# Dilated attention: where the query products wait for the gate, how a head's scores are issued, and where the query copy stands

## The reference

```
def _dilated_mixer(h, k_sh, v_sh, in_w, out_w):
    q, z = jnp.split(h @ in_w, [DIL_Q_WIDTH], axis=-1)      # 3 groups x 8 heads x 128, and 1024
    ...
    for g, (window, dilation) in enumerate(((128, 1), (512, 4), (2048, 16))):
        o, lse = _dilated_window_attention(q[:, :, g], k_sh[:, :, g], v_sh[:, :, g],
                                           window, dilation, slopes[g])
    ...
    wts = jax.nn.softmax(jnp.stack(lses, 2), axis=2)
    o = jnp.einsum("blghe,blgh->blhe", o, wts).reshape(bsz, L, DIL_OUT_WIDTH)
    o = o.astype(h.dtype) * jax.nn.silu(z)
    return o @ out_w
```

## Time and profile before

| | |
|---|---|
| median of 3 runs | 3319.02 us (3318.02 to 3320.58) |
| profiled execution, first to last instruction | 3321.7 us (no other time of it is given) |
| granted TensorE clock, mean | 0.982 |
| TensorE matmuls busy | 3210.1 us (97%) |
| VectorE busy | 2397.5 us (72%) |
| ScalarE busy | 1577.0 us (47%) |
| GpSimd busy | 663.6 us (20%) |
| DMA | 667.85 MB, mean 201 GB/s |

### The profile page before, as it was taken

The page is one execution under the profiler, slowest core; times in us unless marked ns, Lnnn a source line. Parts: engine busy times, 40 slices in busy tenths (PEclk is TensorE's granted clock), DMA queues, the critical chain, the costliest instruction groups (busy, mean ns, idle before and its releaser), DMA issues.

```text
span 3321.7 us, 64507 instructions
## 1 busy us (share of the span) xinstructions
PE 3210.1 (97%) x21980; PEld 2947.2 (89%) x21980; DVE 2397.5 (72%) x3846; ACT 1577.0 (47%) x2226; POOL 663.6 (20%) x635
## 2 busy tenths in 40 slices
PE   8989999999999999999999999999998999999997
PEld 7888999999889998899878879999997879988895
DVE  6665459399878997799999776335898877554455
ACT  4655444433444344433444555545775444344442
POOL 1040039300111001100000116886221111100000
PEclk9999999999999999999999999999999999999998
DMA  6434554666787668866656874666776877755443
GB/s 205 151 98 146 170 164 154 192 207 214 239 267 226 215 218 259 265 200 214 198 178 189 266 249 133 181 189 209 240 236 194 275 235 258 243 188 173 138 128 140
DMA packets 185794, 667.85 MB, mean 201 GB/s; under 512 B 24176, under 2 KB 24400, under 8 KB 184384
## 3 DMA queue, kind: packets, MB, share of 16 engines
q1 hardware_dynamic: 149840, 545.91, 51.9%
q0 software_dynamic: 35824, 120.19, 11.6%
HBM read 663.83 MB, written 2.18 MB: 201 GB/s over the span
## 4 chain that ended last, share of the span: by engine, by line
PE 87%; DVE 5%; issue 3%; ACT 2%; POOL 2%; DMA 0%; DVEq 0%; POOLq 0%; ACTq 0%; SPq 0%
PE PS L562 15%; PE PS L564 15%; PE PS L563 15%; PE PS L906 7%; PE PS L908 7%; PE PS L910 7%; POOL w_lo L476 2%; PE PS L635 2%; PE PS L633 2%; PE PS L634 2%; PE PS L1086 2%; PE PS L1088 2%; PE PS L1090 2%; PE PS L861 1%; PE PS L786 1%
## 5 line engine op out<-in xcount | busy, mean ns | idle before, releaser
L1254 ACT ACTIVATE w_hi<-raw 128x1024 fp32r<-128x1024 f32 x1032 | 1092.9, 1060 | 1574.1 <-PE PS L564 915.0
L1769 DVE TENSOR_TENSOR w_lo<-raw,w_hi 128x1024 fp32r<-128x1024 f32 x872 | 1065.3, 1223 | 577.0 <-ACT w_hi L1254 569.9
L562 PE MATMUL PS<-xt_hi,w_hi 128*128 128x256 f32 x4608 | 1329.8, 289 | 21.7 <-POOL w_lo L476 7.3
L563 PE MATMUL PS<-xt_lo,w_hi 128*128 128x256 f32 x4608 | 1310.0, 284 | 0.0
L564 PE MATMUL PS<-xt_hi,w_lo 128*128 128x256 f32 x4608 | 1309.8, 284 | 0.0
L562 PEld LDWEIGHTS PS<-xt_hi,w_hi 128*128 128x128 f32 x4608 | 890.5, 193 | 32.1 <-issue 22.2
L563 PEld LDWEIGHTS PS<-xt_lo,w_hi 128*128 128x128 f32 x4608 | 890.7, 193 | 0.5
L564 PEld LDWEIGHTS PS<-xt_hi,w_lo 128*128 128x128 f32 x4608 | 890.1, 193 | 0.0
L476 POOL TENSOR_TENSOR w_lo<-raw,w_hi 128x1024 fp32r<-128x1024 f32 x160 | 406.4, 2555 | 372.7 <-ACT w_hi L1254 372.6
L906 PE MATMUL PS<-w_hi,st_hi 128*128 128x512 f32 x1024 | 401.9, 392 | 0.3
L910 PE MATMUL PS<-w_lo,st_hi 128*128 128x512 f32 x1024 | 398.8, 389 | 0.0
(11 more groups left out here) (396 smaller groups left out, 3489.0 us busy)
## 6 DMA issues: line engine op xcount, KB each, us to landing
raw<-in_u_emb SPq DMA_DIRECT2D x256, 512.0 KB, 3.7
raw<-in_v_emb SPq DMA_DIRECT2D x256, 512.0 KB, 4.4
ada<-in_ada_w POOLq DMA_DIRECT2D x240, 256.0 KB, 4.4
raw<-in_xbc SPq DMA_DIRECT2D x96, 512.0 KB, 3.6
raw<-in_z SPq DMA_DIRECT2D x80, 512.0 KB, 3.7
raw<-in_q SPq DMA_DIRECT2D x64, 512.0 KB, 3.5
raw<-in_a_out SPq DMA_DIRECT2D x64, 512.0 KB, 4.2
raw<-in_k SPq DMA_DIRECT2D x48, 512.0 KB, 4.3
```

Of the source, the lines that this page charges most:

```text
L562: pe.matmul(o, w_h, x_h, start=start, stop=False, skip_group_check=True)
L563: pe.matmul(o, w_h, x_l, start=False, stop=False, skip_group_check=True)
L1254: act.activation(w_hi[:, u, :], raw[:, u, :], ACT.Copy).then_inc(hi_done, 1)
L1769: dve.tensor_tensor(w_lo[:, u, :], raw[:, u, :], w_hi[:, u, :].bitcast(F32), ALU.subtract)\
```

## The change

The edits are four. TensorE's waits for the last group of values and for the gate's SiLU move from ahead of the query products to the scores of head 0; ahead of the products stays a wait for the first five groups of values. `head_scores` takes a list of groups and is called twice for each head, with groups 0 and 1 ahead of `head_turn` and group 2 behind it, each call waiting for its own query copies; `head_scored` now counts two for a head, and its two readers are adapted. On ScalarE the query copy moves ahead of the second rounding of its iteration. On VectorE the last head's `head_low` moves one step earlier, behind the fifth `low` of the loop.

```diff
@@ -1152,16 +1152,18 @@
             token_columns(0, FIRST_BODY["z2"], 4, 1, source=shifted_source)
-            pe.wait_ge(sem("v2_out"), 2 * DG)
-            pe.wait_ge(sem("z2_out"), 1)
-
-            def head_scores(h):
-
-                pe.wait_ge(act_free, 2 + ACT_BLOCKS["q2"] + 3 * h + 3)
-                if h:
+            pe.wait_ge(sem("v2_out"), 2 * DG - 1)
+
+            def head_scores(h, groups):
+
+                if h == 0:
+                    pe.wait_ge(sem("v2_out"), 2 * DG)
+                    pe.wait_ge(sem("z2_out"), 1)
+                else:
                     pe.wait_ge(sem("dist_added"), h)
                     pe.wait_ge(sem("pT2_done"), h)
-                for g in range(DG):
+                pe.wait_ge(act_free, 2 + ACT_BLOCKS["q2"] + 3 * h + groups[-1] + 1)
+                for g in groups:
@@ -1210,9 +1212,10 @@
                 if k == 2:
+                    head_scores(h, (0, 1))
                     if h:
                         head_turn(h - 1)
-                    head_scores(h)
+                    head_scores(h, (2,))
@@ -1707,7 +1710,7 @@
                 if i % 3 == 0 and i:
-                    act.wait_ge(sem("head_scored"), i // 3)
+                    act.wait_ge(sem("head_scored"), 2 * (i // 3))
@@ -1742,8 +1745,8 @@
                 if h and k == 0:
                     head_exp(h - 1)
+                head_query(i)
                 high(f + 1 + i // 2, 2 * (i % 2) + 1)
-                head_query(i)
@@ -2640,7 +2643,7 @@
-                dve.wait_ge(sem("head_scored"), h + 1)
+                dve.wait_ge(sem("head_scored"), 2 * h + 2)
@@ -2718,7 +2721,7 @@
                 if i == 3:
                     head_outputs(DH - 1)
-                if i == 5:
+                if i == 4:
                     head_low(DH - 1)
```

## The result

The changed kernel takes 3300.1 us (median of four runs, 3297.3 to 3300.7), where the kernel before takes 3319.8 (median of four runs, 3318.0 to 3323.7) on the same chip. The ratio is 0.9939, with a 95% interval of 0.9927 to 0.9951, so the time fell by 0.5 to 0.7%. The forecast was 3299.3 us in a range of 3294.5 to 3306.5.

What follows compares the result with a forecast made beforehand. TensorE was taken to bound the kernel, carrying 87% of the chain. Gains of 6.9 + 8.2 + 4.6 = 19.7 us off 3319.0 gave 3299.3 us, range 3294.5 to 3306.5.

Steps and rivals of the forecast that it cites:

- The boundary: Gate's last product to first query product: 6.9 us gained, 4.7 of idle and 2.2 of clock.
- The fifth tile's split: Weight tile rounded behind the SiLU: split to about 3059.4, needed at 3063.9, so 4.5 us of slack.
- The heads: Scores in two goes, copy moved up: 8.2 us gained, 1.7 in head 0, 5.7 in heads 1 to 6, 0.8 in head 7.
- where does this stall go: Heads 1 to 6: scores gain 1.48 us, but VectorE's maxima and ScalarE's exponential leave 0.95 us net each.
- The new wait: Before the probabilities' transposes: 0.53 us, from T + 7.99 to T + 8.52, T being the end of a head's third product.
- The copy's move: Query copy ahead of second rounding: delays rounding, split and raw load by 0.27 us in 24 products, hidden by 10.9 us of slack.
- The output tile: Output tile 6, last head's head_low earlier: 4.6 us gained, 2.98 of idle and 1.62 of clock.
- Heads gaining in full without a new wait: Rival: maxima start once scores are there, heads gain 12.05 us in place of 8.2; 3295.5 us, chance 0.15.
- The boundary's other releaser: Rival: the idle at the first query product is not the SiLU's, gain there 0; 3306.2 us, chance 0.06.
- the falling clock among the heads: Rival: clock falls at seven new short waits, 1.6 us each, 11.3 us given back; 3310.6 us, chance 0.03.
- The starved ring: Rival: query products wait for weight tiles, each 0.27 us longer; 3325.5 us, chance 0.02.
- The smaller gain: Head 0, table load with a drain, a switch at about 2.66 us: gain 0.4 instead of 1.7 us.

Runs made afterwards that it cites:

- only_wait: The kernel before with only TensorE's moved waits for the values and the gate's SiLU; ratio 0.9971 against the kernel before.
- gate_copied: The kernel before with a plain copy for the gate's SiLU; gap at the first query product 3.23 us instead of 4.66, no ratio.
- maxima_first: The changed kernel with VectorE taking a head's maxima ahead of the second split of its third product; ratio 0.9927 against the kernel before.
- one_go: The changed kernel with a head's scores in one go behind the transposes, query copy still moved up; ratio 0.9944 against the kernel before.
- copy_behind: The changed kernel with the query copy back behind the second rounding, scores still in two goes; ratio 0.9938 against the kernel before.
- only_low: The kernel before with only the last head's head_low one step earlier; ratio 0.9985 against the kernel before.
- maxima_table: The changed kernel with the maxima ahead of that split and a small exponential at the third query product; 3294.1 us, ratio 0.9915 against the kernel before.
- only_heads: The kernel before with only the scores in two goes and the moved query copy; ratio 0.9970 against the kernel before.
- low_back: The changed kernel with the last head's head_low put back one step later; stretch to output tile 7 22.60 us, no ratio.

## Why the prediction was right

**The boundary, 6.9 us forecast, 6.90 measured.** Both halves hold: the start is one spacing behind the gate's product, and the clock stays at 1.00. only_wait shows that the moved wait does it alone, gate_copied that the SiLU was the releaser. The fifth tile's split runs from 3055.77 to 3057.0 in the changed kernel and its product is due at 3050.11 + 11.5 = 3061.6, so the cover holds with 4.6 us.

**The heads, 8.2 us forecast, 8.88 measured.** The step "where does this stall go" was the right one: of the 1.48 us that the scores gain, a part is lost again to the exponential. Its size was off by little. I put the transposes of the probabilities at T + 8.52 and they come at T + 8.43, a net gain of 1.04 us instead of 0.95 in six heads. In head 0 it is 1.75 for 1.7 (9.14 for 9.17), in head 7 0.92 for 0.8. The new wait, counted as in the prediction from where TensorE is ready (T + 7.94, the start in maxima_first; I had T + 7.99) to T + 8.43, is 0.49 us for 0.53; the 0.34 of the list is not the same measure.

**The copy's move** I treated together with the two goes, as 0 for the weights and as 0.27 us in VectorE's chain. The first holds: TensorE waits for no weights from the boundary on. The second holds as well (the maxima come 0.21 us later, T + 3.04 against T + 2.83), and the runs show what I had not drawn from it. Against the kernel before, the copy moved alone (one_go) takes 7.49 us off the heads, the two goes alone (copy_behind) take off 9.77, and the two together 8.88. The edits do the same work twice, and the second one takes back 0.89.

**The output tile, 4.6 us forecast, 4.57 measured** and 4.56 in only_low. Of it 3.0 is idle; the rest is the clock behind it. The clock fell there in both traces of the kernel before, but that share is not as firm as I wrote (below).

**The sum** is 6.90 + 8.88 + 4.57 = 20.4 us in one pair of traces, and 19.7 us between the medians; the forecast was 19.7. The terms met their stretches; that the medians meet the sum to a tenth is chance, as the runs of one kernel lie 3 to 6 us apart.

**The rivals.** Heads gaining in full without a new wait did not come, but maxima_first makes it come: 12.4 us (178.95 to 166.54) against the 12.05 that I had worked out for that rival. The boundary's other releaser is refuted by gate_copied, the falling clock among the heads by a window of 170 us at 1.00 with eight waits in it. That window also does not bear out, for waits of this length, what the Trainium skill, "TensorE: Matmul & The Clock Gate", section "A second HAM failure mode: psum-queue depth-cycling", says of short idles. The starved ring did not show even in maxima_first, where the second split comes over 4 us later. The smaller gain that I had worked out from the Trainium skill, "ScalarE: Activation LUTs", section "What ACT_TABLE_LOAD costs", was 0.4 us in head 0; it gained 1.75, and the load in maxima_table costs 1.30 us from its start to the next activation, with no drain to be seen.

## What to carry to other kernels

When a stall is removed, follow the chain of every engine to the next point where the bound engine meets it, with the instructions in the order in which each engine has them; here that gave the new wait to within 0.1 us, and its root was a weight split standing ahead of the maxima on VectorE. Two edits that cover the same wait don't add, and the one that delays another engine's queue can cost: try each alone. Take the length of a wait between matmuls from the spacing of their starts, since a list that counts from a modelled end gives less (0.34 for 0.5 us here). Look at what is queued behind a long activation that nobody needs soon, and place the wait for it where its result is first read or its banks first overwritten.

## What was not expected of the hardware

The same idle of 2.9 us before output tile 6 lies in seven traces, and three different clocks followed it. In only_wait (twice) it was 1.00 throughout. In the kernel before (twice) and in gate_copied it fell within the first 0.9 us behind the restart. In only_heads and low_back the first matmul was already at the lower level: the spacing to the next is 0.56 us, where it is 0.30 at full clock. Tile 6 took 2.84 us in the first group, 4.41 to 4.42 in the second, and 4.41 and 5.25 in the third. A fall was also behind the idle of 3.2 us at the boundary in gate_copied, where the first stretch took 22.07 us against 17.27. Each kernel that ran twice gave the same value twice, so two runs can't tell chance from something fixed by what ran before. The edit itself doesn't keep the clock up, since low_back contains it. What decides it stays open. An idle of this length cost itself and 0 to 2.9 us more (in low_back 2.4 us in tile 6 and 0.5 behind it), and the price of one trace should not be carried to a changed kernel as if it were fixed. Behind the idle of 4.7 us at the boundary the clock was low in all four traces that have it, of three kernels (first stretch 24.1 to 24.6 us).
